# One weight sum of a feed-forward pair formed by an adding DMA from GpSimd's queue

## The reference, cut to what matters

```python
D_MODEL, D_FF = 1024, 2816
def swiglu(x, w_in, w_out):
    gate, up = jnp.split(x @ w_in, 2, axis=-1)
    return (jax.nn.silu(gate) * up) @ w_out
x = layer_norm(ALPHA * x + 0.5 * swiglu(x, lw['w_ffn1_in'], lw['w_ffn1_out']), g[0], b[0])
```

## Time and profile before

| What | Value |
|---|---|
| median of three runs | 2752.76 us |
| span of the profiled execution, first to last instruction | 2749.5 us |
| TensorE matmul busy | 2724.5 us, 99% |
| VectorE busy | 1785.8 us, 65% |
| ScalarE busy | 1170.1 us, 43% |
| GpSimd busy | 526.1 us, 19% |
| granted TensorE clock, mean | 0.999 of full |

### The profile page before, as it was taken

One profiled execution on the slowest core, in us unless ns is written; L12 is line 12 of the kernel. 1 busy time (PEld: TensorE's weight loads), 2 busy tenths in 40 slices (PEclk: granted clock), 3 DMA queues, 4 the chain that ended last, 5 costly groups with the idle time before them and its releaser, 6 DMA issues.

```text
span 2749.5 us, 53697 instructions
## 1 busy us (share of the span) xinstructions
PE 2724.5 (99%) x21630; PEld 2634.9 (96%) x21630; DVE 1785.8 (65%) x2824; ACT 1170.1 (43%) x1840; POOL 526.1 (19%) x220
## 2 busy tenths in 40 slices
PE   8999999999999999999999999999999999999998
PEld 8999999799999899999999999987999998999998
DVE  6777665655446478777687776566554364777775
ACT  4343454522345353433454434544223453634344
POOL 0000124134372220000300001331443622100002
PEclk9999999999999999999999999999999999999999
DMA  4323322033362123333223333221233621233332
GB/s 160 102 94 93 100 87 88 27 91 93 93 215 77 46 83 95 91 102 93 90 91 99 94 96 97 81 86 40 85 93 93 214 70 50 83 99 93 93 101 71
DMA packets 75770, 257.93 MB, mean 94 GB/s; under 512 B 10704, under 2 KB 15696, under 8 KB 74256
## 3 DMA queue, kind: packets, MB, share of 16 engines
q1 hardware_dynamic: 68432, 240.66, 28.2%
q10 hardware_dynamic: 7104, 13.94, 1.4%
HBM read 246.70 MB, written 7.87 MB: 93 GB/s over the span
## 4 chain that ended last, share of the span: by engine, by line
PE 96%; DVE 2%; ACT 1%; DVEq 1%; issue 1%; ACTq 0%; DMA 0%; POOL 0%; PEldq 0%
PE PS L490 95%; PE PS L903 0%; DVE O L1777 0%; DVEq L2504 0%; PE PS L1201 0%; ACT LNT L1263 0%; DVEq L2296 0%; DVE LNT L1774 0%; ACTq L1571 0%; DVE P L2304 0%; ACT P L1263 0%; DVE SC L2284 0%; DMA WR<-in_w 0%; ACT Y L1263 0%; ACT WH L1263 0%
## 5 line engine op out<-in xcount | busy, mean ns | idle before, releaser
L480 POOL TENSOR_TENSOR WL<-WR,WH 128x1024 fp32r<-128x1024 f32 x216 | 525.9, 2449 | 2184.4 <-ACT WH L1263 2184.2
L490 PE MATMUL PS<-XH,WH 128*128 128x272 f32 x2464 | 595.7, 291 | 7.3 <-DVE XL L1774 7.3
L490 PE MATMUL PS<-XL,WH 128*128 128x272 f32 x2464 | 587.5, 288 | 0.0
L1263 ACT ACTIVATE WH<-WR 128x1024 fp32r<-128x1024 f32 x450 | 463.9, 1051 | 191.2 <-DMA WR<-in_w 160.4
L490 PEld LDWEIGHTS PS<-XH,WH 128*128 128x128 f32 x2464 | 425.0, 188 | 12.7 <-issue 9.3
L490 PEld LDWEIGHTS PS<-XL,WH 128*128 128x128 f32 x2464 | 425.7, 189 | 0.8 <-issue 0.5
L490 PE MATMUL PS<-XH,WL 128*128 128x272 f32 x2464 | 426.4, 288 | 0.0
L1263 ACT ACTIVATE LNT<-PS 128x272 f32<-128x272 f32 (+5 forms) x350 | 154.0, 450 | 577.2 <-PE PS L490 561.4
L490 PEld LDWEIGHTS PS<-XH,WL 128*128 128x128 f32 x2464 | 353.9, 188 | 0.4
L490 PE MATMUL PS<-HH,WH 128*128 128x272 f32 x1408 | 298.4, 289 | 0.0
L490 PE MATMUL PS<-HL,WH 128*128 128x272 f32 x1408 | 297.3, 288 | 0.0
(11 more groups left out here) (273 smaller groups left out, 5005.8 us busy)
## 6 DMA issues: line engine op xcount, KB each, us to landing
WR<-in_w SPq DMA_DIRECT2D x450, 512.0 KB, 3.6
MRAW<-in_mem ACTq DMA_DIRECT2D x2, 1024.0 KB, 4.9
MKs<-in_memk_in ACTq DMA_DIRECT2D x2, 1024.0 KB, 6.4
MVs<-in_memv_in ACTq DMA_DIRECT2D x2, 1024.0 KB, 9.6
out_mem_k<-MKp ACTq DMA_DIRECT2D x2, 1024.0 KB, 6.0
out_mem_v<-MVp ACTq DMA_DIRECT2D x2, 1024.0 KB, 8.4
out_y<-Y SPq DMA_DIRECT2D x3, 544.0 KB, 3.0
Y<-in_x ACTq DMA_DIRECT2D x2, 544.0 KB, 6.5
```

The lines of the kernel that those rows point to most:

```text
L480: pool.tensor_tensor(WL[s][:, :], WR[s][:, :], WH[s][:, :].bitcast(F32), ALU.subtract).then_inc(lo_ready[s], 1)
L490: return pe.matmul(out, lhsT, rhs, start=start, stop=stop, skip_group_check=True)
L1263: return act.activation(out, in_, func, **kw)
```

## The change

GpSimd's queue now issues, for each of the 72 pairs of the seven-product form, a DMA that reads the second half of the up chunk (256 KB) from HBM again and adds it to the first half of the landed chunk, in place. VectorE no longer forms that sum. GpSimd waits for the semaphore that VectorE's subtraction a11 - a21 raises, because that subtraction reads the first half before it is overwritten. ScalarE's `up_hi` and VectorE's `last_sums` wait for the new semaphore `ff_add`. Because semaphores are few, nine semaphores of the gated attention's output (`o_mm`, `o_ok` and so on) are merged into three that count several steps each, with the same waits and the same order.

```diff
+            sums_at = {CBASE[n] + AT["in", i, 0]: (n, i) for n in ("f1", "f2") for i in range(PLAIN, FC)}
             for l in range(L):
                 for j in range(FIRST if l == 0 else 0, CHUNKS):
+                    if j in sums_at:
+                        name, i = sums_at[j]
+                        s, n = chunk_at(l, j)
+                        pool.wait_ge(*weights_summed(l, name, i, 1))
+                        pool.dma_start(WR[s][:, 0:512], io["w"][n, s][:, 512:1024], accum_op=ALU.add).then_inc(S["ff_add"], 16)
                     if j in by_vector or j in after_norm or (l and j == CBASE["f1"] + 3):
                         continue
...
+        def weights_added(l, name, i):
+
+            return S["ff_add"], 16 * count(l, name, i)
...
                     def up_hi(i):
                         s, n = up_at(l, name, i)
-                        act.wait_ge(*weights_summed(l, name, i, 1))
+                        act.wait_ge(*weights_added(l, name, i))
                         f(WH[s][:, :], WR[s][:, :], ACT.Copy).then_inc(hi_ready[s], 1)
...
                     def first_sums(i):
...
                         settle(ve)
-                        tt(SR[:, 0:512], a11, a21, ALU.subtract)
-                        ve.drain()
-                        tt(a21, a21, a22, ALU.add).then_inc(S["ff_sum"], 1)
+                        tt(SR[:, 0:512], a11, a21, ALU.subtract).then_inc(S["ff_sum"], 1)
 
                     def last_sums(i):
...
                             ve.wait_ge(*product_done(l, name, i - 1, "p6"))
+                        ve.wait_ge(*weights_added(l, name, i))
                         settle(ve)
...
+        def step_of(l, step, engines):
+            for who, steps in engines:
+                if step in steps:
+                    return S[who], l * len(steps) + steps.index(step) + 1
+
+        def gla_out(l, step):
+
+            return step_of(l, step, (("o_pe", ("mm", "ms")), ("o_ve", ("ok", "v", "y", "lo")), ("o_act", ("sq", "r", "hi"))))
...
-                m.then_inc(S["o_mm"], 1)
+                m.then_inc(S["o_pe"], 1)
                 pe.wait_ge(S["ml_rd"], (l + 1) * KC)
                 gate(1)
-                pe.wait_ge(S["o_sq"], l + 1)
+                pe.wait_ge(*gla_out(l, "sq"))
```

More of the change, by code:

```diff
@@ L329, in build @@
                  "rq_sq rq_mm rq_v rq_r ck_in latr_hi lat_ready tanh_r z_in z_mm z_abs z_l B_ok eb_ok kdE kd_sub kd_ok "
-                 "kdt_mm kdt_ok ds_mm ds_rd sb_ok lv_e lv_x lv_E lv_mm lv_sel o_mm o_ok o_sq o_ms o_v o_r o_y o_hi o_lo "
+                 "kdt_mm kdt_ok ds_mm ds_rd sb_ok lv_e lv_x lv_E lv_mm lv_sel o_pe o_ve o_act ff_add "
                  "v_mm v_a v_d qh_mm qh_ok q_mm k_mm qk_ok gv_mm sc_mm mx_ok exp_ok p_ok pt_mm pt_a pt_d pv_mm pv_hi pv_lo "
@@ L1101, in _ @@
                         m = mm(PS[:, 4 + 2 * g + h, 0:TH], BLK, LN_[:, g * T + h * TH:g * T + (h + 1) * TH], True, True)
-                m.then_inc(S["o_ms"], 1)
+                m.then_inc(S["o_pe"], 1)
                 gate(2)
                 gate(3)
-                pe.wait_ge(S["o_lo"], l + 1)
+                pe.wait_ge(*gla_out(l, "lo"))
                 gla(0)
@@ L1651, in _ @@
                 hi_to(cg + 4)
-                act.wait_ge(S["o_ok"], l + 1)
-                f(LN_[:, 0:2 * T], O[:, :], ACT.Square).then_inc(S["o_sq"], 1)
+                act.wait_ge(*gla_out(l, "ok"))
+                f(LN_[:, 0:2 * T], O[:, :], ACT.Square).then_inc(S["o_act"], 1)
                 hi_to(cg + 5)
                 tanh(1)
-                act.wait_ge(S["o_v"], l + 1)
+                act.wait_ge(*gla_out(l, "v"))
                 f(LN_[:, 2 * T:4 * T], LN_[:, 2 * T:4 * T], ACT.Ln)
                 act.drain()
-                f(LN_[:, 2 * T:4 * T], LN_[:, 2 * T:4 * T], ACT.Exp, scale=-0.5).then_inc(S["o_r"], 1)
+                f(LN_[:, 2 * T:4 * T], LN_[:, 2 * T:4 * T], ACT.Exp, scale=-0.5).then_inc(S["o_act"], 1)
                 hi_to(cg + 6)
-                act.wait_ge(S["o_y"], l + 1)
-                f(BH[:, 6 * T:8 * T], O[:, :], ACT.Copy).then_inc(S["o_hi"], 1)
+                act.wait_ge(*gla_out(l, "y"))
+                f(BH[:, 6 * T:8 * T], O[:, :], ACT.Copy).then_inc(S["o_act"], 1)
                 tanh(2)
@@ L1666, in _ @@
                 hi_to(cg + 8)
-                act.wait_ge(S["o_lo"], l + 1)
+                act.wait_ge(*gla_out(l, "lo"))
                 act.wait_ge(S["st_gla"], (l + 1) * 128)
@@ L1981, in first_sums @@
                         (su, nu), (sg, ng) = up_at(l, name, i), gate_at(l, name, i)
-                        a11, a21, a22 = WR[sg][:, 0:512], WR[su][:, 0:512], WR[su][:, 512:1024]
+                        a11, a21 = WR[sg][:, 0:512], WR[su][:, 0:512]
                         ve.wait_ge(landed[su], (nu + 1) * 16)
@@ L2476, in _ @@
                 O3 = O[:, :].rearrange("p (c t) -> p c t", c=2)
-                ve.wait_ge(S["o_mm"], l + 1)
+                ve.wait_ge(*gla_out(l, "mm"))
                 ve.tensor_copy(O3[:, :, 0:NP_], PS[:, 4:6, :])
                 ve.tensor_copy(O3[:, :, NP_:T], PS[:, 6:8, 0:NS])
-                ve.drain().then_inc(S["o_ok"], 1)
-                ve.wait_ge(S["o_ms"], l + 1)
+                ve.drain().then_inc(S["o_ve"], 1)
+                ve.wait_ge(*gla_out(l, "ms"))
                 ve.tensor_scalar(LN_[:, 2 * T:4 * T].rearrange("p (b t) -> p b t", b=4), PS[:, 4:8, 0:TH], 1.0 / 64, EPS,
-                                 ALU.mult, ALU.add).then_inc(S["o_v"], 1)
-                ve.wait_ge(S["o_r"], l + 1)
+                                 ALU.mult, ALU.add).then_inc(S["o_ve"], 1)
+                ve.wait_ge(*gla_out(l, "r"))
                 stt(O[:, :], O[:, :], SMALL[:, SM_GN:SM_GN + 1], LN_[:, 2 * T:4 * T], ALU.mult, ALU.mult)
                 ve.drain()
-                stt(O[:, :], O[:, :], 0.5, SG[:, :], ALU.mult, ALU.mult).then_inc(S["o_y"], 1)
-                ve.wait_ge(S["o_hi"], l + 1)
-                tt(BL[:, 6 * T:8 * T], O[:, :], BH[:, 6 * T:8 * T].bitcast(F32), ALU.subtract).then_inc(S["o_lo"], 1)
+                stt(O[:, :], O[:, :], 0.5, SG[:, :], ALU.mult, ALU.mult).then_inc(S["o_ve"], 1)
+                ve.wait_ge(*gla_out(l, "hi"))
+                tt(BL[:, 6 * T:8 * T], O[:, :], BH[:, 6 * T:8 * T].bitcast(F32), ALU.subtract).then_inc(S["o_ve"], 1)
                 for m in range(KC):
```

## The result

The changed kernel takes 2821.27 us (median of four runs, 2815.54 to 2824.79) against 2752.99 us: ratio 1.0246, 95% interval 1.0232 to 1.0261, 68 us slower. The profiled execution has a span of 2820.0 us, 70.5 us more than before. The sign was right and the time lies in the stated range, but the sum said 22.7 us: a third of what came.

A forecast was written before the change was run, and what follows sets the result against it. TensorE, busy 99% of 2749.5 us at full clock, was taken as the bound. Late landings at four places per feed-forward added 22.7 us, giving 2772.2 us profiled and 2775.5 us for runs; range 2758 to 2828.

The forecast's parts named there:

- the freed VectorE time is worth 0: 72 VectorE additions removed, 49.9 us; `last_sums` is tied to products p6 and p3, so value taken: 0.
- The chain landing, two subtractions, `up_lo`, `CPAIR`, TensorE, at pairs 4, 8, 19 and 20: Late landing delays TensorE through VectorE's queue, four times per place: 5.4, 4.4, 4.2 and 8.7 us, together 22.7 us.
- The allowances: Longest y that costs TensorE nothing: pair 4 2.44, pair 8 2.70, pair 19 2.74, pair 20 1.62 us.
- y = 3.8 us: y: from the end of subtraction a11 - a21 to the start of `last_sums`; taken as 3.8, between 2.7 and 5.2.
- Nearest in what must be read is the 512 KB load: Adding DMA likened to a 512 KB load, 256 KB from HBM plus 256 KB from the slot: 3.6 us.
- An ordinary pair allows 4.48 us: Pairs with an output chunk: VectorE's own round limits y at 4.48 us, so at 3.8 they cost nothing.
- The clock: TensorE's granted clock read as full in every slice, 2.4 GHz; no cost term for it.
- y = 5.2: Upper end, as two transfers in sequence: four places 45.2 us, with ordinary pairs' lateness 80 us in all, 2833.
- Rival B: VectorE becomes the bound in ordinary pairs too, from y = 4.5 on: 2793 to 2833 and more; chance 0.31.
- C: Transfer hidden but for pairs 4 and 20, y of 2.7 or less: 2752.8 to 2758 us; chance 0.13.
- D: VectorE's freed 0.77 us helps at the 12 starts without a chunk, 4.1 us in all: 2748.7; chance 0.04.

The follow-up runs named there:

- e1: Kernel before, with VectorE's 72 additions a21 + a22 left out and nothing in their place: 2751.59 us, ratio 0.9996.
- e12: Changed kernel, with sums of pairs 4, 9, 20, 21 formed by VectorE again and early output sums right behind `CPAIR`: 2751.59 us, ratio 0.9998.
- e4: Changed kernel, with the sums of pairs 4, 9, 20 and 21 (16 of 72) formed by VectorE again: 2773.35 us, ratio 1.0074.
- e2: Changed kernel, with the 72 GpSimd DMAs as plain 256 KB copies, nothing added: 2775.91 us, ratio 1.0081.
- e6: Changed kernel, with the early output sums moved right behind `CPAIR` in VectorE's queue: 2792.53 us, ratio 1.0151.
- e7: Changed kernel, with 14 matmuls of no use at the head of pairs 9, 20 and 21: 2815.24 us, ratio 1.0230.
- e3: Changed kernel, with the adding DMA issued once the up chunk landed and VectorE forming a11 - a21 as (a11 - s1) + a22: 2753.05 us, ratio 0.9999.
- e11: Kernel before, with `up_lo` of pairs 9, 20 and 21 made by GpSimd in place of VectorE: 2755.80 us, ratio 1.0014.

## Why the prediction was wrong

- **What bounds the kernel, and that the freed VectorE time is worth 0**: right. e1 and e12 show it.
- **The chain landing, two subtractions, `up_lo`, `CPAIR`, TensorE, at pairs 4, 8, 19 and 20**: right. TensorE's waits are at these places (27.9 + 7.3 = 35.2 us) and e4 takes them away. The allowances hold: 4.7 - 2.74 = 2.0 us against 2.1 at pair 19. Ahead of pair 4 y was 4.4 to 4.9, mean 4.6, and 4.6 - 2.44 = 2.2 stands against a mean of 1.8 for the four places. Of these 0.4 us 0.2 are the allowance: in the trace of the kernel before, the 16 low matmuls of chunk 7 start at 55.20 us, not at 54.97 as worked out.
- **y = 3.8 us**: the size was off. The median transfer landed after 4.0 us, not 3.6. In the chain of waits at pair 19, below, it lies 0.3 us behind the subtraction, takes 4.24 us, and the third sum starts 0.17 us behind it: 4.7 us. Over the sixteen tight places y was 4.2 to 4.9, once 5.8 (pair 20 of the first feed-forward), mean 4.6. By the prediction's own slope of 16 us per us, 0.8 us is 13 us, and 22.7 becomes 35.5, against 35.2 measured. So this term was mis-sized by 13 us and its mechanism holds. "Nearest in what must be read is the 512 KB load" was too kind; e2 shows plain 2.9 and adding 4.0 us for 256 KB.

```profile
315.58 0.69 DVE SR L1793
316.27 0.28 issue
316.56 4.24 DMA WR<-in_w
```

- **"An ordinary pair allows 4.48 us"**: this step failed. It named two deadlines of an ordinary pair, `CPAIR` and VectorE's own round, and left out the third thing queued behind the wait, the early output sum. Its deadline is what limits pairs 10, 12, 15 and 17: the kernel before allows 3.10 us at pair 12 and, worked out the same way, 3.85 us at pair 10. At these sixteen places y was 4.1 to 4.8, at ten of them under 4.48, and TensorE waited 18.0 us. e4 and e6 show it. The prediction listed what stands behind the wait in both queues and did not put the output sums on the list. Even at the prediction's own y of 3.8 pair 12 would have cost 0.7 us.
- **The clock**: the prediction read the granted clock of the kernel before and took it as fixed. This term was put at nothing. Waits of about two us brought the clock down behind some of them; 70.5 - 53.2 = 17 us of the span's growth are not waiting, an estimated 14 of them are 30.7 us at the lower level, and e7 shows the clock back up where the idle time is filled.
- **The stated range** (2758 to 2828) holds the measured 2821.27 only because its upper end was taken from y = 5.2. What fills it is not what was put there: at the measured y the prediction's two deadlines give 35 us, and the output sums (18 us) and the clock (14 us), which it lacks, bring the rest. That part is luck.
- **Rival B** (VectorE the bound in ordinary pairs, 2793 to 2833) names the right time by a wrong mechanism. VectorE still stands idle ahead of most rounds (11 of 17 in the first feed-forward). e6 removes the ordinary pairs' loss with the same operations on VectorE in another order, and e12 removes all of the loss with 16 additions more on VectorE. Rivals C and D fell.
- **The Trainium skill's formula** (DMA: Bandwidth & Descriptors, "Anatomy of one DMA"), 2.6 us for 256 KB from GpSimd's queue: 2.9 in e2 for the plain transfer, close; 4.0 in the changed kernel for the adding one, which it doesn't cover. The 512 KB load, on which the prediction tried the formula too, is issued from SyncE's queue and not from GpSimd's. That an accumulate reads its destination and writes it later ("Rules for kernel authors") agrees with the 1.1 us between the two, though no run here splits them further.

Left open: the last 3 to 4 of the 70.5 us, which are neither in the waits nor in the lower clock (e4, which has no lower clock, also grows by 4.2 us more than its 17.5 us of waits), and why the clock fell behind some idle pieces and not behind others. Making the transfer start before the subtraction while VectorE keeps its saved operation wasn't tried: the subtraction reads the bytes that the DMA overwrites, so it would need another buffer.

## What to carry to other kernels

A transfer that takes an operation's place is priced by its time from release to landing, not by the engine time it saves, and each thing queued behind the new wait has a deadline of its own: list them all, down to the buffers that they release, and find the shortest. When TensorE is the bound, another engine's freed time is worth nothing until a row shows TensorE waiting for it. A wait of two us on TensorE can cost more than itself, since its clock may be lower for some us afterwards.

## What the hardware showed that was not expected

- An adding DMA of 256 KB from GpSimd's queue into SBUF: 4.0 us from issue to landing (3.5 to 5.3), a plain one 2.9. GpSimd is busy 0.86 us with the issue of the one and 0.54 us with the other.
- 18.9 MB of such transfers beside the weight stream cost nothing (e3: ratio 0.9999; the loads of 512 KB landed after 3.7 us, before 3.6).
- TensorE idle pieces of 2.0 and 2.1 us (ahead of 140.01 and 324.72 us) were each followed by 3.4 us at the lower clock, one of 3.2 us (ahead of 340.24 us) was not.
- A VectorE subtraction of 128x1536 with both inputs in SBUF took 2.44 in place of 1.75 us when it started 0.8 us before the end of a GpSimd subtraction, which itself kept its 2.41 us (e11).
